# Moving values, gate halves and weight splits within the attention loop of a two-layer hybrid encoder

## What is computed

```python
h = rmsnorm(x)
x += W_o( sum_i sigmoid(gate_i(h)) * P_i(branch_i(h)) )
#   A: fox, forgetting attention, 6 heads of 64, strictly causal
#   B: dsa, indexer-sparse attention: I[t,s] = sum_h w[t,h] relu(q_idx[t,h].k_idx[s]),
#      the top k keys are kept, 4 heads of 64 on one key/value head
#   C: mla, low-rank queries, compressed kv latent, rotary key, 6 heads
x += SwiGLU(rmsnorm(x))
```

## Time and profile before

| | |
|---|---|
| median of three runs | 2154.47 us (2154.11 to 2156.47) |
| the profiled execution | 2154.84 us |
| its span in the trace | 2153.0 us (1.84 us lie around it) |
| busy: PE, DVE, ACT, POOL | 2099.4, 1392.0, 968.7, 395.1 us |
| mean granted clock of PE | 0.998 |

### The profile page before, as it was taken

One profiled execution on the slowest core, in us unless ns is written; L12 is line 12 of the kernel. 1 busy time (PEld: TensorE's weight loads), 2 busy tenths in 40 slices (PEclk: granted clock), 3 DMA queues, 4 the chain that ended last, 5 costly groups with the idle time before them and its releaser, 6 DMA issues.

```text
span 2153.0 us, 36860 instructions
## 1 busy us (share of the span) xinstructions
PE 2099.4 (98%) x13616; PEld 1883.8 (87%) x13616; DVE 1392.0 (65%) x2833; ACT 968.7 (45%) x2056; POOL 395.1 (18%) x287
## 2 busy tenths in 40 slices
PE   9999999999999999999999999999999999999999
PEld 8998768878979989989899887787889899899897
DVE  4567875545839838838445678766367497396493
ACT  4236766556425424314232467665663353243241
POOL 1120020200004314314011200203000142242230
PEclk9999999999999999999999999999999999999999
DMA  6233224132332222222232332241423222222222
GB/s 217 78 106 127 83 83 124 59 112 104 119 106 79 79 79 80 88 79 89 77 137 76 110 114 88 79 133 55 149 76 135 72 92 86 79 79 88 72 96 79
DMA packets 90681, 207.83 MB, mean 97 GB/s; under 512 B 20676, under 2 KB 46920, under 8 KB 90184
## 3 DMA queue, kind: packets, MB, share of 16 engines
q1 hardware_dynamic: 90504, 205.48, 28.3%
HBM read 181.50 MB, written 23.95 MB: 95 GB/s over the span
## 4 chain that ended last, share of the span: by engine, by line
PE 89%; DVE 4%; ACT 3%; issue 2%; DVEq 1%; POOL 1%; DMA 1%; SPq 0%; ACTq 0%
PE ps L879 28%; PE ps L925 16%; PE ps L1404 8%; PE ps L1406 8%; PE ps L1405 8%; PE ps L937 6%; PE ps L1096 2%; PE ps L1116 2%; PE ps L995 1%; PE ps L1014 1%; PE ps L1040 1%; PE ps L1210 1%; PE ps L1384 1%; PE ps L1175 1%; POOL rsq L1939 1%
## 5 line engine op out<-in xcount | busy, mean ns | idle before, releaser
L1465 ACT ACTIVATE w_hi<-raw 128x1024 fp32r<-128x1024 f32 (+4 forms) x172 | 171.0, 997 | 398.4 <-PE ps L879 369.4
L1994 DVE TENSOR_TENSOR w_lo<-raw,w_hi 128x1024 fp32r<-128x1024 f32 (+4 forms) x124 | 139.1, 1123 | 187.7 <-ACT w_hi L1465 183.8
L925 PE MATMUL ps<-h_hi,w_hi 128*128 128x320 f32 x768 | 246.8, 321 | 1.5 <-ACT g L1465 1.5
L925 PE MATMUL ps<-h_hi,w_lo 128*128 128x320 f32 x768 | 237.7, 310 | 0.0
L925 PE MATMUL ps<-h_lo,w_hi 128*128 128x320 f32 x768 | 237.6, 309 | 0.0
L1404 PE MATMUL ps<-th_hi,op_hi 128*128 128x320 f32 x640 | 198.1, 310 | 3.8 <-issue 3.8
L1939 POOL TENSOR_TENSOR rsq<-ssq,mhalf 128x12 f32<-128x12 f32 (+3 forms) x56 | 118.0, 2107 | 447.7 <-DVE ssq L2072 385.1
L1406 PE MATMUL ps<-th_hi,op_lo 128*128 128x320 f32 x640 | 198.2, 310 | 0.0
L1405 PE MATMUL ps<-th_lo,op_hi 128*128 128x320 f32 x640 | 198.0, 309 | 0.0
L879 PE MATMUL ps<-w_hi,act_hi 128*128 128x512 f32 x440 | 174.5, 397 | 0.0
L879 PE MATMUL ps<-w_lo,act_hi 128*128 128x512 f32 x440 | 174.4, 396 | 0.0
(11 more groups left out here) (376 smaller groups left out, 5327.5 us busy)
## 6 DMA issues: line engine op xcount, KB each, us to landing
raw<-in_weights SPq DMA_DIRECT2D x212, 512.0 KB, 3.3
gates<-gst SPq DMA_DIRECT2D x72, 160.0 KB, 1.8
g<-gates SPq DMA_DIRECT2D x12, 960.0 KB, 7.0
raw<-in_weights SPq DMA_DIRECT2D x24, 384.0 KB, 3.0
ktb<-in_cache_fox_kt SPq DMA_DIRECT2D x16, 384.0 KB, 4.8
vc<-in_cache_fox_v SPq DMA_DIRECT2D x16, 384.0 KB, 4.1
x_sb<-in_x_prompt SPq DMA_DIRECT2D x8, 512.0 KB, 4.6
out_y_prompt<-x_sb SPq DMA_DIRECT2D x8, 512.0 KB, 3.4
```

Source lines behind the costliest of these rows:

```text
L925: mm = pe.matmul(ps[:, 5, 0:HALF], w[:, kk * P:(kk + 1) * P], h_pair[x][:, kk, half * HALF:(half + 1) * HALF], start=kk == 0 and n == 0, s ...
L1465: return act.activation(dst, src, ACT.Copy, scale=scale)
L1994: dve.tensor_tensor(low[:, 0:width], raw[raw_slot(c)][:, 0:width], high[:, 0:width].bitcast(F32), ALU.subtract).then_inc(lo_made.sem, 1)
```

## The change

- **Values ahead.** Where four prompt items of fox or dsa become due (steps 6, 10, ... 26 and 70, 74, 78, 82), `four_values` is issued at the head of the step, ahead of `scores`, and no longer behind the turn. mla's stay where they are.
- **Gate halves 6 to 17** go from even steps 0 to 22 to odd steps 1 to 23.
- **Chunk splits.** ACT's `hi` of the next chunk leaves `gate_move` and stands behind `exp(s)`, last in the step.
- **Cached values** get a fourth buffer. Streams 5, 6 and 7 use buffers 2, 3 and 1, with loads at SP's steps 5, 7 and 8 of the streams.
- **Banks.** Four early jobs, those of `("dsa", 2)` and of the gate sums, use banks 3 and 4 in place of 6 and 7; others in banks 6 and 7 thereby wait for other jobs. The first index scores get a wait for the gate sums' copies.
- **The end.** DVE makes both halves of `at_dsa`'s split, in two column pieces; ACT's copy is gone.

```diff
+EARLY = {JOB[_p] + _k: 3 + _k for _p in (("dsa", 2), ("gate_sums", 0)) for _k in range(2)}
-    BANK.append(5 if _j in THIRD else 6 + (_j - sum(_k < _j for _k in THIRD)) % 2)
+    BANK.append(5 if _j in THIRD else EARLY[_j] if _j in EARLY else 6 + (_j - sum(_k < _j for _k in THIRD)) % 2)
...
-        GATE_AT.append(_n - _n % 2 if _n < I_FOXS else _n + 1 - _n % 2 if I_MLA <= _n < I_MLAS - 4
+        GATE_AT.append(_n + 1 - _n % 2 if _n < I_FOXS else _n + 1 - _n % 2 if I_MLA <= _n < I_MLAS - 4
                        else _n + (_n == I_MLAS - 3))
...
-        vc = [...] + [home("vc2", [P, 2, FH * HD], F32, "bias")]
+        vc = [...] + [home("vc2", [P, 2, FH * HD], F32, "wqb"), home("vc3", [P, 2, FH * HD], F32, "bias")]
...
+                    if step == I_FOXS + 5:
+                        sp.wait_ge(tp_done.sem, tp_done.at(L, JOB["mla_expand", TT - 1] + 3))
+                        own_wait(sp, sp_tick)
+                        sp.dma_start(vc[2][:, :, :], past("fox_v", 5)).then_inc(vc_in[2].sem, 16)
                     if step == I_FOXS + 7:
                         sp.wait_ge(tp_done.sem, tp_done.at(L, JOB["mla_turn", TT - 1] + 4))
                         own_wait(sp, sp_tick)
-                        sp.dma_start(vc[2][:, :, :], past("fox_v", DECB - 1)).then_inc(vc_in[2].sem, 16)
+                        sp.dma_start(vc[3][:, :, :], past("fox_v", 6)).then_inc(vc_in[3].sem, 16)
+                    if step == I_FOXS + 8:
+                        sp.wait_ge(it_pv.sem, it_pv.at(L, I_FOXS + 4))
+                        own_wait(sp, sp_tick)
+                        sp.dma_start(vc[1][:, :, :], past("fox_v", 7)).then_inc(vc_in[1].sem, 16)
                     b = step - (I_FOXS + 2)
-                    if 2 <= b < DECB - 1:
+                    if 2 <= b < 5:
...
                 def index_scores(i):
                     if i == 0:
+                        pe.wait_ge(tp_out.sem, tp_out.at(L, JOB["gate_sums", 0] + 2))
...
                 for step in range(N_ITEMS + 6):
+                    ahead = 3 <= step < N_ITEMS + 3 and VALUED[step - 3] == step - 3 and ALL_ITEMS[step - 3][0] in ("fox", "dsa")
+                    if ahead:
+                        values(step - 3)
                     if step < N_ITEMS:
                         scores(step)
...
-                    if 3 <= step < N_ITEMS + 3 and not last_four:
+                    if 3 <= step < N_ITEMS + 3 and not last_four and not ahead:
                         values(step - 3)
...
                     copy(dst, ps[:, 5, 0:HALF]).then_inc(g_moved.sem, 1)
-                    if half:
-                        if k != GATE_LAST:
-                            hi(C_GATE + 2 + m, m % 2)
+
+                def gate_next(k):
+                    if k % 2 and k != GATE_LAST:
+                        hi(C_GATE + 2 + k // 2, k // 2 % 2)
...
                     if step < N_ITEMS:
                         exp(step)
-                act.wait_ge(tp_out.sem, tp_out.at(L, JOBS))
-                copy(h_hi[:, 6:8, :], at_dsa[:, :, :]).then_inc(at_hi.sem, 1)
+                    if step:
+                        for k in GATES_IN[step - 1]:
+                            gate_next(k)
                 hi(C_OUTS + 1, 1)
...
-                dve.wait_ge(at_hi.sem, at_hi.at(L, 1))
-                at_rest(6, 2, at_dsa)
+                dve.wait_ge(w_used.sem, w_used.at(L, C_OUTS))
+                dve.wait_ge(it_out.sem, it_out.at(L, I_DSAS))
+                for cols in (slice(0, SEQ), slice(SEQ, NTOK)):
+                    if cols.start:
+                        dve.wait_ge(tp_out.sem, tp_out.at(L, JOBS))
+                    dve.tensor_copy(h_hi[:, 6:8, cols], at_dsa[:, :, cols])
+                    dve.drain()
+                    last = dve.tensor_tensor(h_lo[:, 6:8, cols], at_dsa[:, :, cols], h_hi[:, 6:8, cols].bitcast(F32), ALU.subtract)
+                last.then_inc(at_lo.sem, 1)
```

More of the change, by code:

```diff
@@ L391, in build_program @@
         gate_new = home("gate_new", [102, P], BF16)
-        vc = [home(f"vc{k}", [P, 2, FH * HD], F32, "vc", 3072 * k) for k in range(2)] + [home("vc2", [P, 2, FH * HD], F32, "bias")]
+        vc = [home(f"vc{k}", [P, 2, FH * HD], F32, "vc", 3072 * k) for k in range(2)] + [home("vc2", [P, 2, FH * HD], F32, "wqb"), home("vc3", [P, 2, FH * HD], F32, "bias")]
         kpe = home("kpe", [P, TT, ROPE])
@@ L483, in build_program @@
         g_in, g_ready, acc_made, mix_half = sig("g_in", 16 * GATE_KEPT), sig("g_ready", KD), sig("acc_made", KD), sig("mix_half", KD)
-        at_hi, at_lo, vd_made = sig("at_hi", 1), sig("at_lo", 3), sig("vd_made", 1)
+        at_lo, vd_made = sig("at_lo", 3), sig("vd_made", 1)
         rows_free = sig("rows_free", 2)
@@ L496, in build_program @@
         lfr_made, grow_made = sig("lfr_made", 1), sig("grow_made", 1)
-        vc_in = [sig(f"vc_in{k}", 16 * (DECB // 2 - k)) for k in range(2)] + [sig("vc_in2", 16)]
+        vc_in = [sig(f"vc_in{k}", 16 * n) for k, n in enumerate((3, 3, 1, 1))]
         ktb_in, ctb_in = ([sig(f"{n}{k}", 16 * DECB // 4) for k in range(4)] for n in ("ktb_in", "ctb_in"))
@@ L1127, in values @@
                     if kind == "foxs":
-                        s = 2 if t == DECB - 1 else s
-                        pe.wait_ge(vc_in[s].sem, vc_in[s].at(L, 16 * (t // 2 + 1) if s < 2 else 16))
+                        s = (0, 1, 0, 1, 0, 2, 3, 1)[t]
+                        pe.wait_ge(vc_in[s].sem, vc_in[s].at(L, 16 * (1, 1, 2, 2, 3, 1, 1, 3)[t]))
                     if i == I_MLAS:
@@ L1317, in _ @@
                     last_four = step in (I_FOXS + 2, I_MLAS + 2, I_DSAS + 2)
-                    if last_four:
+                    if last_four and not ahead:
                         values(step - 3)
@@ L1738, in _ @@
                 gate_move(1)
+                gate_next(1)
                 index_relus(0)
@@ L1744, in _ @@
                 gate_move(3)
+                gate_next(3)
                 fox_moves(2)
@@ L1749, in _ @@
                 gate_move(5)
+                gate_next(5)
                 for step in range(N_ITEMS + 6):
```

## The result

The changed kernel takes 2192.31 us (median of four runs, 2188.52 to 2195.35), the kernel before 2154.29 in the same comparison: a ratio of 1.0173, 95% interval 1.0159 to 1.0187. That is 38.0 us slower, where 20.6 was forecast. The range ended at 2192: the median lies 0.3 above it, the ratio on the 2154.47 of before gives 2191.7, so the result is at the range's edge. The profiled execution took 2194.38 us, with a span of 2192.6.

What follows compares the result with a forecast made beforehand. PE, busy 98% of the span, was taken to bound the kernel, so every new PE wait lengthens it. Terms summed to +20.6 us on the profiled 2154.84, 2175.4, forecast as a median of 2175; range 2149 to 2192.

Steps and rivals of the forecast that it cites:

- part 1: Gate halves 6 to 17 in odd steps: +26 us pair waits, +5 at step 0, -2.5 for index products.
- Pair waits, +26: First branch (fox): second turn waits for ACT's copy out of bank 3; 1.2 us for 11 pairs a layer, +26 us.
- The empty step 0, +5: Loop start: no gate half fills step 0, so PE waits for DVE's index split; 2.8 us a layer, +5 us.
- The index products, -2.5: First branch: with the gate behind the index turn, index products no longer wait for `qs`; -2.5 us.
- Values ahead, -1.8 and +2: Values before scores: fewer array-shape changes, 0.1 us for nine quads a layer, -1.8; two pairs uncovered in third branch, +2.
- The late split, +4 and -1.5: Chunk's high half behind exp: 0.4 us for five chunk changes a layer, +4; second branch's four waits shrink, -1.5 us.
- Cached values, -4.5: Four buffers for fox's cached values: PE's waits of 1.7 and 1.6 us and the half clock behind them shrink; -4.5 us.
- Banks, -4.4: Ahead of the loop: banks 3 and 4 for four early jobs remove transposes' waits for ACT's moves; -4.4 us.
- The end, -1.7: `at_dsa` split made by DVE alone, in pieces: both waits of L937 for `h_lo` go; -1.7 us.
- Rival C: The clock falls too: pairs idle over 1.5 us may each cost another 1.5, +15, giving 2190 us; chance 0.1.
- Rival A: Second turn hardly late: a pair costs 0.5 us (+11), step 0 nothing, gains come whole; faster, 2145 us; chance 0.2.
- Rival B: No change: pairs cost 0.9 us, DVE holds the loop in both orders, waits only move; 2154.5 us; chance 0.08.

Runs made afterwards that it cites:

- parity_only: The kernel before with only gate halves 6 to 17 moved from even to odd steps; 2184.59 us, ratio 1.0131.
- small_three: The kernel before with only the banks for four early jobs, the fourth cached-values buffer and DVE's split at the end; 2143.85 us, ratio 0.9945.
- values_only: The kernel before with only four_values issued ahead of the scores; 2167.32 us, ratio 1.0051.
- late_only: The kernel before with only the next weight chunk's split moved behind exp; 2164.56 us, ratio 1.0050.
- undo_parity: The changed kernel with gate halves 6 to 17 back in even steps; 2182.41 us, ratio 1.0122.
- three_bank4: The small_three kernel with turns of items 4n+3 of mla and dsa in PSUM bank 4; 2135.73 us, ratio 0.9909 to the kernel before.

## Why the prediction was right or wrong

The direction was right, and so was the mechanism of its largest part: alone, the parity costs 27.4, where part 1 had 26 + 5 - 2.5 = 28.5. The size of the whole was about half, and the result lies at the range's edge. By its own steps:

- **Pair waits, +26.** Ten a layer, 11.0 and 11.3 us in the two layers (sums of the idle times at L1105 in fox): 22. With the 0.17 that a wait costs beyond its idle time, these twenty pairs come to +26. That the term came out so well is in part luck: eleven pairs at 1.2 were counted, and there are ten at 1.3.
- **The empty step 0, +5.** 2.77 in either layer: +5.5. **The index products, -2.5**: gone. Not in the sum: the wait for `qa`, 2.3 us more in parity_only.
- **Values ahead, -1.8 and +2: the step that failed.** Alone they cost 11.5 us. I had priced the changes of array shape, and the pairs uncovered in dsa, and not asked what the values themselves wait for: they need the copy of the turn right ahead of them. The prediction also named the value that the term would have by the Trainium skill (page "TensorEngine Tiling (Array Packing)", section "Key Properties"), 0, with a sum 1.8 higher. No run measures the changes of shape by themselves, and 11.5 us of waits hide them; but the missing row is in the changed kernel:

```profile
248.92 1.75 PE L1125 MATMUL ps<-probs_t,p_v 128*64 128x128 f32 x28
250.60 0.70 PE L1023 MATMUL ps<-kf,qf 64*128 64x256 f32 x4
```

The 28 values take 1.68 us to the row-strip scores behind them, and took 1.68 to the full-array gate (242.46 to 244.14). So a change from column to row strips is no dearer than one to the full array, and three changes in place of four is the better reading. The quads are ten a layer, not nine.

- **The late split, +4 and -1.5.** Alone 8.8. The chain that I summed for fox cost nothing there on balance (0.0 to turn 20); the loss is in dsa and its streams, where steps are short and ACT's and DVE's queues hold the split ahead of what PE needs next. I had priced fox and mla only.
- **Cached values, -4.5.** -2.7 to turn 31, with the clock, in small_three. In the changed kernel the gap's place was taken by waits for `av` of 0.77, 0.81 and 1.04 us in either layer, and the clock fell there in layer 0 (331) but not in layer 1. From turn 20 to turn 31 the layers win 1.8 and 1.5 us all the same, but the wait for `qa` (1.15 a layer before) is gone in the same stretch; what the buffers gave there stays open.
- **Banks, -4.4**: -5.3. **The end, -1.7**: -2.2.
- **The clock.** Rival C, to which I gave 0.1, took part: PE's busy time is 8.8 us longer, where the sum had counted on some 2 less. So of the 19 us by which the profiled execution goes beyond the sum, about 11 are the clock, as an estimate, and the rest waits. Within the four runs of the changed kernel the span goes with the clock: 2186.7 at 0.995, 2193.6 at 0.990. The statement of the Trainium skill that an idle engine falls back to the slow clock (page "TensorE: Matmul & The Clock Gate", Part 1) fits the rows; which gap is followed by a fall differs from run to run and layer to layer (2.77 us at 183.13 was not, the same gap at 1267.54 was).
- **Rival A** fell: in ten pairs of each layer second turns started after 0.84 to 1.78 us of idle time, never within 0.6 of the first. **Rival B** fell with it.

Taken alone against before, the parts are +27.4 (parity), +11.5 (values), +8.8 (late split) and -11.5 (the three small ones): +36.2, next to 38.0 measured together. That these agree is luck, for the parts aren't independent: without the parity the other three cost 25.2, where their sum is 8.8. PE's idle and busy times in the profiled executions tell the two reasons apart (us more than in the kernel before):

| run | idle | busy |
|---|---|---|
| parity_only | +24.1 | +6.4 |
| values_only | +16.7 | -1.3 |
| late_only | +9.9 | -0.2 |
| small_three | -5.6 | -4.9 |
| undo_parity | +21.6 | +8.3 |
| changed kernel | +30.8 | +8.8 |

The waits of the other three add up: 16.7 + 9.9 - 5.6 = 21.0, next to 21.6 in undo_parity. What doesn't is the busy time, -6.4 against +8.3, and with it the clock: PE is busy for 39.5 us at the 1.2 GHz level in undo_parity, for 12.7 and 12.9 in values_only and late_only. So the surplus, 15.3 us in these executions, is nearly all the clock: 45% of the time at that level makes some 14 of it. Parity, on the other hand, shares waits with the rest: 24.1 alone, but only 9.2 more on top of undo_parity, as odd gate halves cover the values, whose waits fall from 17.4 to 3.9.

## What to carry to other kernels

When long work of the bottleneck engine is moved, ask what it covered where it stood: here one gate half of 3.6 us hid a relu, a copy and a bank's release, and moving it by one step cost 27 us, 14 of which stayed when it stood between the turns again, one step late. Ask of every instruction that is moved ahead what it reads and who makes that; an order that is safe in one plan (values behind an odd gate half) waits in the other. A second bank for the one transpose that is late (three_bank4) gained 8.1 us, where each reordering tried alone here lost. Look at busy time too: where it grows at the same count of matmuls, the waits also cost clock.

## What was unexpected of the hardware

Eight stretches at the 1.2 GHz level stand in the changed kernel's trace in place of three, behind gaps of 1.0 to 2.8 us, in a kernel whose PE is 96% busy. The same 13616 matmuls are busy for 2108.2 us in place of 2099.4. Which gap is followed by a fall isn't fixed by its length: 1.30 us at 1529.43 was, 2.77 at 183.13 was not. The clock also differs between executions of one kernel: nine of the kernel before have spans from 2148.7 at a mean clock of 1.000 to 2156.9 at 0.997, and five of values_only 2160.4 at 1.000 to 2168.4 at 0.996. At 1.000 the two kernels differ by 11.7 us, about what the medians say (11.5), so that difference is not the clock's.
